# Feed-forward of the second block: where VectorE makes the low parts of the activations, and where ScalarE splits the next up panel

## The reference

```python
def conv_ffn(x, w_up, conv_w, conv_b, w_down):      # D_FF_2 = 2816, w_up: 1024 x 5632
    u = x @ w_up
    c = u.shape[-1]
    u = lax.conv_general_dilated(u, conv_w[:, None, :], window_strides=(1,),
                                 padding=[(CONV_WIDTH - 1, 0)],
                                 dimension_numbers=('NWC', 'WIO', 'NWC'),
                                 feature_group_count=c) + conv_b
    a, b = jnp.split(u, 2, axis=-1)
    return (jax.nn.gelu(a) * b) @ w_down
...
    x = layer_norm(DN_ALPHA * x + y, ln2_g[l], ln2_b[l])
```

## Time and profile before

| | |
|---|---|
| median of three runs | 3487.1 us |
| the profiled execution | 3489.91 us, its span 3488.1 us |
| TensorE matmul, busy | 3404.4 us (98%), 16680 matmuls |
| VectorE, busy | 1527.5 us (44%) |
| ScalarE, busy | 1410.8 us (40%) |
| GpSimd, busy | 1450.6 us (42%) |
| granted clock of TensorE, mean over the span | 0.994 |
| bytes moved by DMA | 298.52 MB, mean 86 GB/s |

### The profile page before, as it was taken

One profiled execution on the slowest core, in us unless ns is written; L12 is line 12 of the kernel. 1 busy time (PEld: TensorE's weight loads), 2 busy tenths in 40 slices (PEclk: granted clock), 3 DMA queues, 4 the chain that ended last, 5 costly groups with the idle time before them and its releaser, 6 DMA issues.

```text
span 3488.1 us, 45848 instructions
## 1 busy us (share of the span) xinstructions
PE 3404.4 (98%) x16680; PEld 2774.0 (80%) x16680; DVE 1527.5 (44%) x2498; ACT 1410.8 (40%) x2056; POOL 1450.6 (42%) x1100
## 2 busy tenths in 40 slices
PE   8999999999999999999999999999999999999998
PEld 6788878887788878887768887787777788877786
DVE  5623332225623432227852444434488424344435
ACT  4734232224735332223462444333345524343333
POOL 4333544444333544444432343444443323434442
PEclk9999999999999999999999999999999999999999
DMA  4222222222222222222211222222222122222221
GB/s 146 73 73 85 97 85 97 96 96 99 73 73 96 98 85 97 97 96 86 85 53 69 73 88 73 97 96 89 92 74 85 49 73 73 97 73 90 91 96 60
DMA packets 43814, 298.52 MB, mean 86 GB/s; under 512 B 4816, under 2 KB 5456, under 8 KB 8592
## 3 DMA queue, kind: packets, MB, share of 16 engines
q1 hardware_dynamic: 41696, 291.52, 23.5%
q10 hardware_dynamic: 1968, 4.94, 0.4%
HBM read 294.34 MB, written 2.10 MB: 85 GB/s over the span
## 4 chain that ended last, share of the span: by engine, by line
issue 52%; POOL 32%; PE 13%; DVE 1%; ACT 1%; POOLq 0%; DMA 0%; DVEq 0%; ACTq 0%; SPq 0%
POOL w_lo L339 32%; PE ps L470 4%; PE ps L472 4%; PE ps L471 4%; POOL own_lo L339 1%; DMA w_raw<-stream 0%; POOLq L345 0%; DVE arena L1764 0%; PE ps L555 0%; ACT arena L1203 0%; DVE x L1800 0%; POOLq L338 0%; DVE arena L1788 0%; ACT y_hi L1222 0%; ACT x L1563 0%
## 5 line engine op out<-in xcount | busy, mean ns | idle before, releaser
L339 POOL TENSOR_TENSOR w_lo<-w_raw,w_hi 128x512 fp32r<-128x512 f32 x1064 | 1407.1, 1354 | 1994.8 <-ACT w_hi L1018 1994.8
L470 PE MATMUL ps<-x_hi,w_hi 128*128 128x512 f32 x2608 | 1033.9, 396 | 8.4 <-POOL w_lo L339 5.8
L472 PE MATMUL ps<-x_hi,w_lo 128*128 128x512 f32 x2608 | 1016.6, 390 | 0.0
L471 PE MATMUL ps<-x_lo,w_hi 128*128 128x512 f32 x2608 | 1016.3, 390 | 0.0
L1018 ACT ACTIVATE w_hi<-w_raw 128x1024 fp32r<-128x1024 f32 x532 | 531.5, 1048 | 463.6 <-PE ps L472 463.6
L470 PEld LDWEIGHTS ps<-x_hi,w_hi 128*128 128x128 f32 x2608 | 490.0, 188 | 132.5 <-issue 24.2
L472 PEld LDWEIGHTS ps<-x_hi,w_lo 128*128 128x128 f32 x2608 | 490.0, 188 | 103.9
L471 PEld LDWEIGHTS ps<-x_lo,w_hi 128*128 128x128 f32 x2608 | 490.2, 188 | 100.0 <-issue 2.4
L470 PE MATMUL ps<-y_hi,w_hi 128*128 128x512 f32 x1248 | 490.6, 393 | 16.8 <-DVE x L1800 13.0
L471 PE MATMUL ps<-y_lo,w_hi 128*128 128x512 f32 x1248 | 487.3, 390 | 0.0
L472 PE MATMUL ps<-y_hi,w_lo 128*128 128x512 f32 x1248 | 487.2, 390 | 0.0
(11 more groups left out here) (215 smaller groups left out, 3231.6 us busy)
## 6 DMA issues: line engine op xcount, KB each, us to landing
w_raw<-stream SPq DMA_DIRECT2D x274, 1024.0 KB, 4.8
x<-x_t SPq DMA_DIRECT2D x4, 512.0 KB, 5.8
rotary<-rot ACTq DMA_DIRECT2D x4, 512.0 KB, 3.5
y_t<-x SPq DMA_DIRECT2D x8, 256.0 KB, 2.2
ct<-consts ACTq DMA_DIRECT2D x2, 770.0 KB, 5.4
arena<-pos ACTq DMA_DIRECT2D x2, 256.0 KB, 3.8
vec<-vectors ACTq DMA_DIRECT2D x4, 116.0 KB, 2.0
ct<-consts ACTq DMA_DIRECT2D x1, 128.0 KB, 3.5
```

The costliest lines, as they stand in the source:

```text
L339: ins = nc.gpsimd.tensor_tensor(low(c)[:, o:o + S], RAW[:, c % 2, o:o + S], high(c)[:, o:o + S].bitcast(F32), ALU.subtract)
L470: pe.matmul(ps, wh, xh, start=(k == 0), stop=False)
L471: pe.matmul(ps, wh, xl, start=False, stop=False)
L472: return pe.matmul(ps, wl, xh, start=False, stop=last)
```

## The change

On VectorE, in the second block (kt = 2), the two low parts of group g + 1 leave `up` of group g + 1, except in group 0 of a layer, and come in `down` of group g: the first behind adds 0 and 1 and ahead of add 2, the second behind add 2 and ahead of add 3. They are computed by the new function `hidden_lo` in the same way and with the same wait.

On ScalarE, in the second block, the split of the next panel (`next_panel`: the a panel of the group after the next one, or, at the end, the last down panel) leaves `down` of group g and comes in `up` of group g + 1, behind that group's last read of an up tile (L1203) and ahead of the two high parts (L1222). For the last group it stays in `down`. What is computed, the number of instructions and the order of the panels stay the same. TensorE's, GpSimd's and SyncE's programs aren't touched.

```diff
--- ScalarE
                     if kt == 2:
+                        if not (gi == 0 and gc == 0):
+                            next_panel(gc - 1, gi, i)
                         for m in range(2):
                             act.wait_ge(hid_ready, base_h + 2 * g + m + 1)
...
                             act.activation(YH[:, 2 * buf + m, :], AR[:, 6 + m, :], ACT.Copy).then_inc(hid_hi, 1)
 
                 def down(gc, gi, i):
+                    if downs == 2:
+                        hi_down(gc, gi, i, 1)
+                    if kt == 4 or (gi == 0 and gc == groups - 1):
+                        next_panel(gc, gi, i)
+
+                def next_panel(gc, gi, i):
                     last = gi == 0 and gc == groups - 1
                     nxt_up = not (gi == 0 and gc >= groups - 2)
-                    if downs == 2:
-                        hi_down(gc, gi, i, 1)
                     if nxt_up:
                         hi_up(gc + 2, gi, i, 0)
                     elif not last:
--- VectorE
-                        for m in range(2):
-                            dve.wait_ge(hid_hi, base_h + 2 * g + m + 1)
-                            dve.tensor_tensor(YL[:, 2 * buf + m, :], AR[:, 6 + m, :], YH[:, 2 * buf + m, :].bitcast(F32),
-                                              ALU.subtract).then_inc(hid_lo, 1)
+                        if first:
+                            hidden_lo(gc, gi, i, 0)
+                            hidden_lo(gc, gi, i, 1)
+
+                def hidden_lo(gc, gi, i, m):
+
+                    g, k = gc + gi * i, 2 * (gc % 2) + m
+                    dve.wait_ge(hid_hi, base_h + 2 * g + m + 1)
+                    dve.tensor_tensor(YL[:, k, :], AR[:, 6 + m, :], YH[:, k, :].bitcast(F32), ALU.subtract).then_inc(hid_lo, 1)
 
                 def down(gc, gi, i):
                     g = gc + gi * i
                     for m in range(8):
+                        if kt == 2 and m in (2, 3) and not (gi == 0 and gc == groups - 1):
+                            hidden_lo(gc + 1, gi, i, m - 2)
                         dve.wait_ge(down_full, CREDIT + base_d + 8 * g + m + 1)
                         dve.wait_ge(down_added, CREDIT + base_d + 8 * g + m - 7)
                         dve.tensor_tensor(X[:, m, :], X[:, m, :], PS[:, 4 + m % 4, :], ALU.add).then_inc(down_added, 1)
```

## The result

The changed kernel takes 3494.7 us (median of 14 runs, 3492.8 to 3497.8), the kernel before in the same comparison 3487.5 us: ratio 1.0019, 95% interval 1.0012 to 1.0027. A second comparison on another occasion gave 3493.1 against 3490.0 us, 1.0010 (1.0001 to 1.0019). It is slower by 3 to 7 us; the forecast was 3.8 us slower. The first median lies 0.6 us above the band that the prediction called no change (up to 3494.1), the second inside it.

The account below looks back on a forecast made before the run. TensorE, busy for 98% of the span, bounds the kernel, so only its waits count. First add later (1.6 us) plus third add (2.2) gave +3.8 us on the median of 3487.1: 3490.9 us, range 3477 to 3498.

Parts of the forecast that it names:

- 0.95 us a group at the first add, 19.1 us in all, and no more to be won: Second block's down product: TensorE waits on VectorE's late add into x, 0.95 us in each of 20 groups, 19.1 us.
- The low parts out of the way, by themselves, free the first add: VectorE: the first add, right behind the second product, ends at 2264.76, 0.74 us before TensorE asks, so no wait.
- The split and GpSimd start 0.68 and 1.80 us behind the conv read: ScalarE's moved split starts 0.68 us, GpSimd's first panel piece 1.80 us, behind the group's last conv read.
- The products take turns: VectorE's two products alternate with GpSimd's pieces at SBUF, 1.69 us a turn; first add 0.08 us later, 1.6 us in all.
- A tie for low part 0: Low part 0 and GpSimd's fourth piece issue together; losing delays the third add, 0 to 4.4 us, half taken: 2.2.
- The panel is in time: GpSimd ends at 2268.1 to 2268.7, before TensorE wants the panel at 2271.9; tight only had the wait gone.
- the wait goes: Rival, 12%: the products do not meet GpSimd, TensorE's wait on the first add vanishes, all 19.1 us come: 3468.0 us.
- Longer turns: Rival, 15%: at both products VectorE and GpSimd hand over whole operations, 1.98 us a turn; +10.2 us, 3497.3 us.
- The first product slips in ahead: Rival, 8%: VectorE's first product starts before GpSimd's first piece, first add 0.40 us earlier; 8.0 us won, 3479.1 us.

Follow-up runs that it names:

- both_places: The changed kernel with ScalarE's split waiting for the group's last tap and the low parts ahead of adds four and five; 3471.3 us, ratio 0.9944.
- dve_alone: The changed kernel with ScalarE's split back in `down`, leaving VectorE's part of the change alone; 3483.8 us, ratio 0.9980 to the kernel before.
- product_psum: The changed kernel with products reading PSUM and the arena instead of two arena tiles, TensorE waiting for the product before rewriting that bank; 3470.1 us, ratio 0.9943.
- act_alone: The changed kernel with the low parts back ahead of the adds, leaving ScalarE's part of the change alone; 3599.7 us, ratio 1.0320 to the kernel before.
- dve_alone_later: VectorE's part alone (split back in `down`), with the low parts ahead of adds four and five; 3493.8 us, ratio 1.0012 to the kernel before.

## Why the prediction was right

Point by point, with the times after less the 1.94 us by which that group lies later:

- *0.95 us a group at the first add, 19.1 us in all, and no more to be won*: both_places has it all, with groups of 32.64 us and 18.7 us less.
- *The low parts out of the way, by themselves, free the first add*: dve_alone.
- *The split and GpSimd start 0.68 and 1.80 us behind the conv read*: 0.69 and 1.81.
- *The products take turns*: product one was to end at 2264.04 and ended at 2264.06, product two 2265.73 and 2265.76, the first add 2266.33 and about 2266.35. The wait is 0.75 instead of 0.65: 0.10 us more a group, where 0.08 stood in the sum.
- *A tie for low part 0*, 2266.85 against GpSimd's 2266.83: it was issued at 2266.88 against 2266.86 and lost, and in all 20 groups, 0.01 to 0.03 us behind, it did so. This is the term that was mis-sized. The sum took half of at most 0.22 us; 0.21 came. So the groups cost 20 × (0.10 + 0.21) = 6.2 us instead of 3.8, close to the upper end of the sum (6.0); the rest of the 7.2 us of the first comparison lies outside them, and that the second comparison's 3.1 us is near 3.8 is chance. The working put the two 0.02 us apart, less than it could tell. But all 20 groups repeat the same sequence, so one end or the other, 1.6 or 6.0 us, was to be expected, and half was a middle between them that neither outcome would have given.
- *The panel is in time*: GpSimd ended at 2268.14 in these times, and no wait on it is in a group. Once the wait on the add is gone and the split stays late, the panel is late: TensorE waits for it 0.42 us (dve_alone), about the 0.45 us that GpSimd loses to low part 1. The prediction had called this case tight, without that turn.
- The rivals: *the wait goes* needed products that do not meet GpSimd. That is what product_psum makes of it, and it then wins 20.0 us (3470.1 beside 3490.1 for the kernel before), where that rival stood at 19.1. *Longer turns* fell: a turn took 1.70 us here and 1.67 to 1.70 in act_alone, not 1.98. *The first product slips in ahead* did not come; its remedy, a later GpSimd, is what both_places does on purpose.

The Trainium skill (SBUF — State Buffer, section "Who interferes with whom") states that a VectorE instruction with two inputs in SBUF contends with a GpSimd instruction that reads SBUF, and one with at most one, outside its two-port modes, does not. product_psum agrees, with 1.27 us for two products instead of 2.87. That the other side is blocked for a whole instruction (section "SBUF: two separate sides", which the prediction weighed) does not agree in size: VectorE ended 0.55 us behind the piece that held it, less than its own 0.68.

## What to carry to other kernels

When an operation is moved earlier, look at which engine it sets off, and what lies under that engine's work afterwards: here the split fell into ScalarE's idle time, and the GpSimd work that it released took back what the edit on VectorE had won. Count for each VectorE operation how many of its inputs lie in SBUF; those with two are best kept away from GpSimd's work where a deadline stands behind them, and put beneath it where none does. Two edits that are good together need not be good in the same form: the low parts ahead of adds four and five help with the early split and hurt without it.

## What the runs showed of the hardware

- A turn costs both sides, and not the same. VectorE ends 0.55 us behind the piece that held it, sooner than its own 0.68 us: it lost 0.5 to 1.1 us in the changed kernel and 0.24 in both_places, 0.13 less than was left of GpSimd's piece. GpSimd loses 0.45 us.
- With work queued on both, the two alternate: in act_alone four VectorE operations directly behind each other end 1.67 to 1.70 us apart, with one piece of GpSimd's between each two.
- At 0.01 to 0.03 us apart, the one that is issued first goes first: GpSimd in all 20 groups of the changed kernel, VectorE at 1115.31 us of the trace of before. Where both are shown at the same time, 104.91 us, GpSimd did.
- A short wait of TensorE costs more than its length. For waits listed as 0.42, 0.65, 0.75 and 0.87 us (dve_alone, before, the first wait after, dve_alone_later) a group was 0.71, 0.95, 1.04 and 1.16 us longer than 32.64: 0.3 us on top each time. Of that, 0.16 is only how a wait is listed, from the end of a matmul (0.39 us behind its start) and not from when the next could have started (0.23); about 0.14 is the refill.
- Behind a wait of 4.08 us the granted clock was 0.52 instead of 1.00, and 8 to 13 matmuls took 0.20 us more each: 1.6 to 2.6 us a group, over 40 us in act_alone.
